# The first eight V rows of an expert stage, gathered from U row 18 on, each behind the query weights that held its slot

## What is computed

```python
def peer_ffn(h, w_peer_q, sub_keys, peer_u, peer_v):
    q = (hf @ w_peer_q).reshape(n, PEER_HEADS, 2, D_KEY // 2)
    s1 = jnp.einsum('nhd,kd->nhk', q[:, :, 0], sub_keys[0])
    s2 = jnp.einsum('nhd,kd->nhk', q[:, :, 1], sub_keys[1])
...
    top_s, top_pos = lax.top_k(cand_s, PEER_TOPK)
    idx = jnp.take_along_axis(cand_i, top_pos, axis=-1)
    gate = jax.nn.softmax(top_s, axis=-1)
    u = jnp.take(peer_u, ib, axis=0)
    a = jnp.einsum('nhkd,nd->nhk', u, hb)
    w = gb * jax.nn.gelu(a, approximate=False)
    vv = jnp.take(peer_v, ib, axis=0)
    return jnp.einsum('nhk,nhkd->nd', w, vv)
```

## Time and profile before

| | |
|---|---|
| median of three runs | 2779.6 us |
| the profiled execution | 2779.34 us, span 2777.5 us |
| TensorE, VectorE, GpSimd busy | 89%, 51%, 38% of the span |
| gathers and other DMAs issued by GpSimd | 723.48 MB, 64.7% of 16 engines' span |
| HBM read in all | 906.92 MB, mean 329 GB/s |
| granted TensorE clock, mean | 0.967 |

### The profile page before, as it was taken

How to read it: one execution, slowest core, us unless ns; L and a number is a source line. 1 busy time by engine, 2 the same in 40 slices (tenths; PEclk the granted TensorE clock), 3 DMA queues, 4 the chain that set the end, 5 groups by cost and what they waited for, 6 DMA issues and landing times.

```text
span 2777.5 us, 27969 instructions
## 1 busy us (share of the span) xinstructions
PE 2467.6 (89%) x9187; PEld 1581.7 (57%) x9187; DVE 1425.9 (51%) x2283; ACT 350.6 (13%) x774; POOL 1060.4 (38%) x952
## 2 busy tenths in 40 slices
PE   9999999979999999999997777776999597777777
PEld 6788888868766678888885323332344142332333
DVE  2465566963322223001367877885554656555543
ACT  2111000002222211000112011111011011111100
POOL 1165566020122200000055656655444564455542
PEclk8999999989999999999998999998999899999999
DMA  5599999694799965446388999999999999999998
GB/s 166 175 333 335 321 342 354 199 340 148 256 349 345 353 234 185 150 137 212 122 327 332 414 414 412 418 419 421 421 412 419 411 411 417 421 417 422 421 421 371
DMA packets 305613, 914.97 MB, mean 329 GB/s; under 512 B 15706, under 2 KB 196018, under 8 KB 236724
## 3 DMA queue, kind: packets, MB, share of 16 engines
q0 software_dynamic: 122304, 723.48, 64.7%
q1 hardware_dynamic: 183188, 190.03, 21.0%
HBM read 906.92 MB, written 6.56 MB: 329 GB/s over the span
## 4 chain that ended last, share of the span: by engine, by line
PE 29%; DMA 23%; DVE 16%; issue 14%; POOL 14%; POOLq 3%; ACT 1%; DVEq 0%; SPq 0%; ACTq 0%
DMA sb_bregion<-in_peer_u_dram,sb_ring 12%; PE ps L719 12%; PE ps L731 6%; DMA sb_mkv<-in_peer_u_dram,sb_ring 4%; PE ps L632 4%; POOL sb_ring L432 3%; DMA sb_S<-in_peer_u_dram,sb_ring 3%; DVE sb_bregion L1914 3%; POOL sb_mkv L432 3%; PE ps L821 2%; POOL sb_wring L533 2%; POOL sb_bregion L533 2%; POOLq L423 2%; DVE sb_mkv L1914 2%; POOL sb_S L533 1%
## 5 line engine op out<-in xcount | busy, mean ns | idle before, releaser
L976 PE MATMUL ps<-sb_wring,sb_ring 128*128 128x512 f32 x992 | 458.1, 612 | 85.2 <-DMA sb_wring<-in_peer_v_dram,sb_ring 84.4
L632 PE MATMUL ps<-sb_hT,sb_wring 128*128 128x264 f32 x1792 | 409.6, 390 | 4.4 <-DMA sb_wring<-in_w_in_dram 2.1
L1914 DVE CUSTOM_DVE_ANT_0 sb_bregion<-sb_bregion,sb_rows 128x2048 f32<-128x2048 f32 x128 | 293.5, 2293 | 212.0 <-DMA sb_bregion<-in_peer_u_dram,sb_ring 204.6
L976 PEld LDWEIGHTS ps<-sb_wring,sb_ring 128*128 128x128 f32 x992 | 186.9, 194 | 353.7 <-issue 267.6
L719 PE MATMUL ps<-sb_hT,sb_wring 128*128 128x264 f32 x1536 | 367.2, 390 | 14.2 <-ACTq L1121 12.6
L632 PEld LDWEIGHTS ps<-sb_hT,sb_wring 128*128 128x128 f32 x1792 | 341.1, 192 | 64.5 <-issue 3.2
L719 PEld LDWEIGHTS ps<-sb_hT,sb_wring 128*128 128x128 f32 x1536 | 288.2, 191 | 78.0 <-issue 29.2
L976 PE MATMUL ps<-sb_oreg,sb_ring 128*128 128x512 f32 x496 | 233.8, 622 | 77.7 <-DMA sb_oreg<-in_peer_v_dram,sb_ring 57.5
L976 PE MATMUL ps<-sb_hT,sb_ring 128*128 128x512 f32 x496 | 230.7, 611 | 55.2 <-DMA sb_hT<-in_peer_v_dram,sb_ring 48.1
L533 POOL DMA_INDIRECT sb_bregion<-in_peer_u_dram,sb_ring x132 | 181.6, 1376 | 213.6 <-DVEq L1311 177.6
L976 PEld LDWEIGHTS ps<-sb_oreg,sb_ring 128*128 128x128 f32 x496 | 95.4, 199 | 215.1 <-issue 154.1
(11 more groups left out here) (370 smaller groups left out, 2818.3 us busy)
## 6 DMA issues: line engine op xcount, KB each, us to landing
sb_wring<-in_w_in_dram SPq DMA_DIRECT2D x52, 2048.0 KB, 12.5
sb_ring<-in_cache_k_dram POOLq DMA_DIRECT2D x64, 512.0 KB, 6.6
sb_mkv<-in_cache_k_dram POOLq DMA_DIRECT2D x64, 512.0 KB, 6.5
sb_mkv<-in_cache_v_dram POOLq DMA_DIRECT2D x48, 512.0 KB, 7.2
sb_rows<-in_cache_v_dram POOLq DMA_DIRECT2D x47, 512.0 KB, 7.1
sb_wring<-in_w_mem_kv_dram SPq DMA_DIRECT2D x8, 2048.0 KB, 8.4
sb_wring<-in_w_o_dram SPq DMA_DIRECT2D x8, 2048.0 KB, 8.3
sb_S<-in_cache_v_dram POOLq DMA_DIRECT2D x22, 512.0 KB, 7.3
```

Of the source, the lines that this page charges most:

```text
L632: last = mm(ps[:, (2 * r + c) % 4, 0:NT], wring[:, r, k, c * P:(c + 1) * P], rhs[:, k, :], start=(k == 0), stop=(k == KC - 1))
L976: last = mm(ps[:, 4 * t + q, :], diag[:, k % 4, :], e_slots[v % ER][:, q * 512:(q + 1) * 512], start=False, stop=q_stop, skip_group_check= ...
L1914: st(V.tensor_tensor_reduce(out=u_slots[n % UR], in0=u_slots[n % UR], in1=h2, scale=1.0, scalar=0.0, op0=ALU.mult, op1=ALU.add, accum_out= ...
```

## The change

Only the schedule is changed: up to U35 a list says after which U row each of V0 to V7 is gathered (V0 after U18, V1 after U20, V2 and V3 after U28 and U29, V4 to V7 after U31 to U34), and from U36 on 236 more (V8 to V243) are spread evenly over the U rows that are left. The waits before V0, V2, V4 and V6 stay as they are.

```diff
+        FIRST_V = [18, 20, 28, 29, 31, 32, 33, 34]
+
         def v_before(n):

-            return max(0, (n - V_LEAD + 1) * (V_SLOTS - V_LEFT) // (U_SLOTS - V_LEAD))
+            if n < V_LEAD + 2:
+                return sum(first <= n for first in FIRST_V)
+            return ER + (n - V_LEAD - 1) * (V_SLOTS - V_LEFT - ER) // (U_SLOTS - V_LEAD - 2)
```

## The result

| | median | against before |
|---|---|---|
| before | 2778.44 us (11 runs, 2771.96 to 2780.77) | - |
| after | 2783.64 us (11 runs, 2781.08 to 2788.76) | ratio 1.0026 (95%: 1.0017 to 1.0034) |

By the medians the change costs 5.2 us, by the ratio 7.2 (4.7 to 9.4); the forecast said 5.5. Both are under 0.3% of the time, so the rest of the argument goes by the trace and by variants more than by this one difference. The profiled executions differ by 4.2 us: 2783.54 (span 2781.8) against 2779.34.

What follows compares the result with a forecast made beforehand. In the expert stage the DMA engines were taken as the bound, 2.49 us per gather, so empty-queue time is lost. The sum -2.5 - 2.5 + 0.5 + 10.0 = +5.5 gave a forecast of 2785.0 us, range 2777.0 to 2789.5.

Steps and rivals of the forecast that it cites:

- (a): Waits for query-weight chunks before V0, V2, V4 and V6: none holds, cost 0.
- (b): V0 and V1 near the hole at 1480 us: V0 pays for itself, V1 fills 2.49 us; gain 2.5 us.
- (c): V2 to V7, where the queue ran short between dots 28 and 35: gain 2.5 us.
- (d): V8's wait for a slot is covered by 4 us; routing after dot 35 costs 0.5 us, bounds 0 and 3.
- R3: Rival, chance 0.11: slower by GpSimd's issue, 2790 us; decides once V8's issue is over 13 us after U32's landing.
- (e): V144, now behind U168, waits for the sample addition after dot 166; only four rows in flight, 10.0 us more lost.
- R1: Rival, chance 0.14: the hold at V144 is bridged or doesn't arise, only the front counts; faster, 2774.5 us.
- R2: Rival, chance 0.05: V0 too falls into the hole, front gives 8, hold costs 8; no effect, 2779.5 us.

Runs made afterwards that it cites:

- e5: The kernel before with V0 alone moved to behind U18: 2779.15 us, ratio 1.0002 (0.9988 to 1.0015).
- e6: The kernel before with V0 alone moved to behind U20: 2775.97 us, ratio 0.9986 (0.9977 to 0.9995).
- e1: The changed kernel's first eight V rows, but the lead over before shrinks to 0 by U150: 2773.02 us, ratio 0.9981 against before.
- e3: The changed kernel with the sample output added after dot 163 instead of dot 166: 2775.46 us, ratio 0.9990 against before.
- e8: e1 with V0 to V3 behind U20 to U23 and V4 to V7 behind U31 to U34: 2768.99 us, ratio 0.9975 against before.
- e7: e1 with V7 behind U35 instead of U34: 2773.93 us, ratio 0.9983 against before.
- e11: e1 with V0-V3 behind U20-U23, V4-V6 behind U31-U33, V7 behind U35, and the sample addition after dot 163: 2764.37 us, ratio 0.9944 against before.
- e2: The kernel before up to U123, then a lead of two V rows, so V144 stands behind U168: 2785.61 us, ratio 1.0027 against before.
- The halves: The change split in two against before: the new front alone (e1), -5.3 us, and the late lead of two V rows alone (e2), +7.5 us.
- e9: The kernel before with a lead of one V row from U126 on, given back after the hold: 2785.90 us, ratio 1.0026 against before.

## Why the prediction was right, and where it was lucky

A slip first that changes nothing: the DMA row stays at 9 from the 23rd slice on, the one that begins at 1528 us, not from the 22nd.

**(a) Query waits, 0: right.** V0 to V7 were issued at 1456.4, 1464.6, 1502.3, 1507.9, 1511.6, 1515.9, 1520.2 and 1526.4, each 0.30 us behind the item before it. None waited for TensorE.

**(b) V0 pays for itself, V1 gains 2.5: V0 right, V1 somewhat too much.** U24 went out 39.0 us after U16, 3.0 more than before, where 2.5 was forecast. Two rows more (5.0 us) for 3.0 us are a gain of 2.0, forecast 2.5. U24's distance in e5 and e6 shows that the place alone decides: ahead of U19 V0 costs what it brings, behind U20 it is won. The hole was to shrink by 2; added up by shares it went from 9.2 to 8.2.

**(c) V2 to V7, 2.5: about right, 2.0.** From dot 28 (1510.51) to dot 35 are 13 rows in 32.65 us, 2.51 a row; before it was 3.11. Not all of this is (c), for the norm weights moved. Dot 27 in before, then dots 27 and 28 in after, VectorE in order of time, and SP's load of the norm weights in after:

```profile
1502.63 2.29 DVE L1914 CUSTOM_DVE_ANT_0 sb_bregion<-sb_bregion,sb_rows 128x2048 f32<-128x2048 f32 x1 [0.71 <-DMA sb_bregion<-in_peer_u_dram,sb_ring]
```

```profile
1504.44 2.29 DVE L1918 CUSTOM_DVE_ANT_0 sb_bregion<-sb_bregion,sb_rows 128x2048 f32<-128x2048 f32 x1 [0.79 <-DMA sb_bregion<-in_peer_u_dram,sb_ring]
1510.51 2.29 DVE L1918 CUSTOM_DVE_ANT_0 sb_mkv<-sb_mkv,sb_rows 128x2048 f32<-128x2048 f32 x1 [3.76 <-DMA sb_mkv<-in_peer_u_dram,sb_ring]
```

```profile
1499.53 0.34 SPq L367 DMA_DIRECT2D sb_rows<-in_norm_w_dram  x1
```

In the terms of the ledger after is 2.0 ahead at dot 27, 0.7 behind at dot 28 and 4.0 ahead at dot 35. The 2.7 between the first two are the norm weights (136 rows of 8 KB, 1.11 MB or 2.6 us; the prediction had 1.09 and 2.5): in before SP loads them 3.0 us after U28's gather is issued (1500.47 and 1497.50), in after 0.3 us after it (1499.53 and 1499.28), so in before they fall between dots 28 and 35. That they are the cause is inferred from size and place. So of the 4.0 us at dot 35, 2.0 belong to (b) and 2.0 to (c), where 5.0 were forecast together.

**(d) V8 covered, routing 0.5: first half right, second too small.** V8 waited 6.38 us and went out 10.5 after dot 32's start (1528.31), forecast some 9, below R3's 13. I had let the routing after dot 35 cost almost nothing. By shares the windows from 1560 to 1575 miss 1.4 us, by bytes (256, 356 and 395 GB/s against 421) 3.0. By landings the ledger falls from 4.0 at dot 35 to 3.2 at dot 41 (1571.70; 1561.17 in before), 0.8 us; in e1, e3 and e8, which also have V7 behind U34, the same fall is 1.6, 1.4 and 0.9, and in e7 and e11, with V7 behind U35, there is none. So the missing ninth row is the cause, and the term was about 1, not 0.5.

The step that failed: I let the eight rows behind U35 begin with dot 35. The dot started 1543.16 and the queue ran dry at about 1560.6, as 1 us windows of after show:

```profile
1560.00:1561.00 1.00, 1.00 (x4) 0.38 (x3) 0.81 (x3) 0.00 (x0) 1.00 (x1) 1.00 0.63 262
1561.00:1562.00 1.00, 1.00 (x4) 0.52 (x3) 1.00 (x1) 0.00 (x0) 0.70 (x2) 1.00 0.16 66
1562.00:1563.00 1.00, 1.00 (x4) 0.42 (x3) 1.00 (x1) 0.40 (x1) 1.00 (x1) 1.00 1.02 172
```

That is 17.4 us, not 19.9. The dot had been waiting for its row, so its start shows when the landing was seen, and by then the next row had been running for over 2 us. The new rows, on the other hand, came sooner than forecast: the first bytes after U40's issue (1559.04) came at about 1562.0, 3.0 us later and not 4.2. The first error alone would have made the hole 2.5 us wide; the second gave half of that back. The Trainium skill ("DMA: Bandwidth & Descriptors", section Anatomy of one DMA) gives some 2.0 us of fixed cost for a transfer and puts most of it behind the last byte; the 2.5 us that 17.4 falls short of 19.9, an estimate for what lies between a row's last byte and its dot, are of that size.

**(e) The hold, +10.0: mechanism right, size 8.2 to 8.9.** e2 has it without the front, e3 has the front without it. The chain from dot 166 to V144 was forecast at 15.6 us, as before, and was 15.45. Of the rest, V144's gather was taken at before's length, 2.55 us beside a dot, and took 0.94, as no dot ran: that is 1.6 of the 1.8 us by which U169 came earlier (24.3 after dot 166, forecast 26.1). My own row for a gather alone had this number; the hold empties VectorE too, which I had not followed through. This is the largest single error of the sum.

The transfer time of the Trainium skill (same page and section), an estimate of 2.0 us and 4.8 for two rows, would bring U169 6.8 us after V144's issue; the trace has 8.9. It stays too short here, though by less than at U24 in before.

**The sum.** The forecast was -5.0 (b, c) + 0.5 (d) + 10.0 (e) = +5.5. The ledger has -4.0 at dot 35, +1.9 from there to dot 166 (0.8 of it (d), the rest in no term), +8.2 at the hold and -0.6 after it: +5.5 again, against +5.2 and +7.2 measured. The front was 1.0 too large, the way to dot 166 1.4 too small and the hold 1.8 too large. The mechanism and the size of its two main terms were right, but that the sum is right to a fraction of a us is luck.

**The rivals.** R1 fell: the hold was not bridged. It is right for e1 and e3, where it doesn't arise. R2 fell: V0 gives nothing ahead of U19. R3 fell: the point from which it decides was not reached, and dots 28 to 35 came at 2.51 us a row although V2, V4, V5 took 2.0 to 2.7 us of GpSimd. Its loss after dot 35 did come, from the cause under (d). R3's sign, a second hole near 1560, was seen, but e7 gives it another cause. Against the bound of 0.2% (5.6 us) after lies above it with the ratio (7.2, interval 4.7 to 9.4) and just below with the medians (5.2); the forecast had put 0.44 and 0.47 there.

**What stays open.** The halves add to less than the whole (+2.2 against +7.2). The ledger shows 1.9 us of the front's gain gone between dot 35 and dot 166; (d) accounts for 0.8 of that by landings. e1 and e3 lose 2.1 and 1.7 on the same way, e7 and e8 nothing. What (d) doesn't account for has no cause shown: other routings cost one to three us in both kernels, but not the same ones (by bytes after misses 3.4 us from 1800 to 1900, before 1.9 from 2000 to 2100), and I have one profiled execution of each.

## What to carry to other kernels

When issues stand in one in-order queue, count for each hold how many transfers are in flight behind the event that ends it: here 8 rows (19.9 us) nearly bridge it, 4 don't, and every V row of lead takes two away. A lead built up for one gap must be given back before a hold that is fixed elsewhere, or the hold must move along; and a filler belongs behind the transfer that the next step waits for, not ahead of it. When the length of a queue is counted from the start of a compute step that waited for its row, the next row is already on its way; here that was 2.5 us. In a bandwidth-bound stage read the GB/s row and 5 us windows: the tenths row showed nothing of a hole that cost more than the whole front gained.

## What the runs showed of the hardware

- A gather of 1.049 MB took 0.94 us of GpSimd with no dot beside it and mostly 2.2 to 3.0 us beside one: 0.94 (V144 of after), 2.77 (of e9, beside U169's dot). What is fixed is not its length but its end: of the 160 gathers of before that begin while a dot runs, 152 end 0.79 to 0.86 us after that dot. A VectorE operation of the same length with one input in PSUM does not do this: U170's gather began 0.7 us into the addition (2216.71, 2.28 us) and took 0.93. The Trainium skill ("SBUF — State Buffer", section SBUF: two separate sides) tells of a port pair that VectorE and GpSimd share as an exclusive lock; a gather that is held to the end of a dot with both inputs in SBUF, and not by an addition from PSUM, agrees with such a lock, but no run was made to test it.
- A dot that waits for its row starts over 2 us after the DMA engines went on to the next row (17.4 us of eight rows' 19.9 were left at dot 35's start).
- TensorE had stood idle for 34.83 us before the zeroing of after; the granted clock was 0.50 from 2220 to 2225, its level of 1.2 GHz, 0.89 in the next window and then 1.00. In e3_add_early, 21.37 us idle, the zeroing at 2204.33 met 0.50 too, and the clock was 1.00 from 2210 on. The zeroing took 6.36 us at 0.50 where a V row of the same eight matmuls takes half of 7.03 at 1.00, so an estimate of 2.8 us of the chain from dot 166 to V144 is the lower clock, in before as in after.
